# Expert gathers of a decoder layer in chunks of 8 slots: another distance between the two streams, twelve diagonals, other work moved between the first slots

## The reference

```
q = h @ w_q                                  # 8 heads, 2 parts of 128
s = q . sub_keys                             # 128 keys per head and part
s1, i1 = top_k(s[part 0], 16); s2, i2 = top_k(s[part 1], 16)
top_s, e = top_k of the 256 sums s1 + s2     # 16 experts per head, e = i1 * 128 + i2
g = softmax(top_s)
act = gelu(u_tab[e] . h)
y = sum over 8 x 16 experts of (g * act) * v_tab[e]
out = x1 + gate2 * y
```

## Time and profile before

| | |
|---|---|
| median of 3 runs | 1356.63 us |
| the profiled execution | 1362.06 us |
| its span | 1360.4 us |
| busy: PE / DVE / ACT / POOL | 1060.8 / 705.3 / 244.3 / 655.7 us |
| mean granted clock of PE | 0.884 of full |
| read from HBM | 377.55 MB, of them 302 MB for the 576 gathers |
| first gather / last gather asked | 486.75 / 1335.20 us |

### The profile page before, as it was taken

One profiled execution on the slowest core, in us unless ns is written; L12 is line 12 of the kernel. 1 busy time (PEld: TensorE's weight loads), 2 busy tenths in 40 slices (PEclk: granted clock), 3 DMA queues, 4 the chain that ended last, 5 costly groups with the idle time before them and its releaser, 6 DMA issues.

```text
span 1360.4 us, 12692 instructions
## 1 busy us (share of the span) xinstructions
PE 1060.8 (78%) x3429; PEld 568.0 (42%) x3429; DVE 705.3 (52%) x1695; ACT 244.3 (18%) x552; POOL 655.7 (48%) x787
## 2 busy tenths in 40 slices
PE   6898888996899979657776768776857777777797
PEld 3346666664676766323322323232322333233243
DVE  3157453886142366768467466473772774334421
ACT  1011121123201103111121211211202112112021
POOL 3333334331000043667666667566666666666651
PEclk9798898998999999879878988788889888987799
DMA  7653241885043474899999999999999999999993
GB/s 237 203 191 113 73 134 46 285 289 146 1 153 133 179 305 141 330 370 369 366 370 368 367 365 367 355 368 374 365 376 379 353 368 370 364 382 352 373 372 118
DMA packets 126411, 379.87 MB, mean 279 GB/s; under 512 B 14284, under 2 KB 23624, under 8 KB 126356
## 3 DMA queue, kind: packets, MB, share of 16 engines
q0 software_dynamic: 89408, 312.89, 61.3%
q1 hardware_dynamic: 36948, 66.29, 14.6%
HBM read 377.55 MB, written 1.59 MB: 279 GB/s over the span
## 4 chain that ended last, share of the span: by engine, by line
PE 65%; issue 15%; DVE 8%; another core or an unknown queue 5%; ACT 4%; DMA 2%; POOL 1%; SPq 0%; DVEq 0%; ACTq 0%
PE twoD L825 19%; PE twoD L827 17%; PE twoA L513 6%; PE twoA L779 4%; PE twoD L730 2%; PE twoA L490 2%; PE twoA L653 1%; PE twoD L608 1%; PE twoA L450 1%; PE twoD L720 1%; PE twoD L696 1%; PE twoD L466 1%; DMA big<-w_ada 1%; DVE big L1593 1%
## 5 line engine op out<-in xcount | busy, mean ns | idle before, releaser
L825 PE MATMUL twoD<-big 128*128 128x512 f32 x576 | 344.7, 684 | 204.6 <-issue 184.5
L951 POOL DMA_INDIRECT big<-peer_v,oT x288 | 273.0, 948 | 179.4 <-issue 79.9
L827 PE MATMUL twoD<-big 128*128 128x512 f32 x576 | 327.5, 653 | 0.0
L938 POOL DMA_INDIRECT big<-peer_u,oT x210 | 199.6, 950 | 247.9 <-DVEq L1551 163.9
L825 PEld LDWEIGHTS twoD<-big 128*128 128x128 f32 x576 | 114.7, 213 | 391.3 <-issue 387.7
L1182 ACT ACTIVATE big<-ctab,oT 128x128 f32<-128x128 f32 x288 | 110.1, 399 | 640.0 <-remote 257.9
L827 PEld LDWEIGHTS twoD<-big 128*128 128x128 f32 x576 | 122.4, 213 | 163.7 <-issue 163.7
L1593 DVE CUSTOM_DVE_ANT_0 big<-big,twoA 128x1024 f32<-128x1024 f32 x115 | 137.3, 1217 | 69.9 <-DMA big<-peer_u,oT 56.0
L1593 DVE CUSTOM_DVE_ANT_0 big<-big,twoD 128x1024 f32<-128x1024 f32 x95 | 114.6, 1215 | 40.4 <-DMA big<-peer_u,oT 23.7
L513 PE MATMUL twoA<-hT,big 128*128 128x288 f32 x448 | 114.3, 415 | 0.0
L513 PEld LDWEIGHTS twoA<-hT,big 128*128 128x128 f32 x448 | 86.0, 194 | 24.2 <-issue 0.8
(11 more groups left out here) (285 smaller groups left out, 1004.3 us busy)
## 6 DMA issues: line engine op xcount, KB each, us to landing
big<-w_ada SPq DMA_DIRECT2D x12, 2048.0 KB, 9.2
big<-w_in SPq DMA_DIRECT2D x5, 2048.0 KB, 8.1
big<-w_in SPq DMA_DIRECT2D x9, 1024.0 KB, 11.3
big<-peer_w_q SPq DMA_DIRECT2D x4, 2048.0 KB, 8.0
big<-peer_v,oT POOLq DMA_INDIRECT x288
big<-cache_v POOLq DMA_DIRECT2D x64, 64.0 KB, 2.1
big<-w_out SPq DMA_DIRECT2D x2, 2048.0 KB, 7.8
big<-cache_k POOLq DMA_DIRECT2D x56, 64.0 KB, 3.6
```

Source lines behind the costliest of these rows:

```text
L825: pe.matmul(acc[0][:, :], diag[:, j % NDG, :], row[:, 0:512], start=(s == 0), stop=(s == SLOTS[t] - 1), skip_group_check=True)
L827: mm = pe.matmul(acc[1][:, :], diag[:, j % NDG, :], row[:, 512:D], start=(s == 0), stop=(s == SLOTS[t] - 1), skip_group_check=True)
L938: pool.indirect_dma_start(urows[i % NU], None, peer_u, bass.IndirectOffsetOnAxis(ap=eidx[:, t, s:s + 1], axis=0)).then_inc(u_in[i % NU], 16)
L951: pool.indirect_dma_start(vrows[j % NV], None, peer_v, bass.IndirectOffsetOnAxis(ap=eidx[:, t, s:s + 1], axis=0)).then_inc(v_in[j % NV], 16)
```

## The change

Sizes: chunks of 8 slots (`CHUNK`) in place of 16 for gelu, weighting and `w_ready`; NU 11 to 10, NV 10 to 11, NDG 4 to 12 (the further diagonals lie in tensors that are no longer in use). The v stream runs behind the u stream by `min(18, 10 + i // 8, 8 + (287 - i) // 3)` slots: 10 at first, 18 from slot 64, and down to 8 at the last slot.

Order: the gate2 rows, the later scores and the token rows become 15 pieces `late(k)` that PE makes before v slots 6, 8, ..., 34, in the order g2, scores, token rows, and ACT copies after the diagonal six slots later. h of tiles 1 and 2 is turned before slot 64. `gelus(c + 1)` stands behind diagonal 8c + 7, `exps` behind the gelu of every fourth chunk, and `normalise` inside `weigh`, which DVE comes to at i = 11, 19, ...

Storage: the last group of q weights has a place of its own, so its load no longer waits for the second group's use; the stores of the convolution state and the load of the bias stand earlier in SP's order.

```
-        NU, NV = 11, 10
+        NU, NV = 10, 11
-        LAG = 24
-        HEAD = PTOP
+        LAG, NEAR = 18, 8
+        HEAD, CHUNK = PTOP, 8
+        NDG = 12
...
+        slot_of[-1] = 4
+        shares = {0: (0, 2, 3), 1: (1,), 2: (0, 2), 3: (0, 3), 4: (4,)}
...
+        LATE = list(range(6, 6 + 2 * 15, 2))
+        H2_REST = 64
...
             for j, (t, s) in enumerate(slots):
+                if j in LATE:
+                    late(LATE.index(j))
+                if j == H2_REST:
+                    pe.wait_ge(a_free, A.n)
+                    turn_h2(1)
+                    turn_h2(2)
...
-            for i in range(ROUNDS + LAG):
-                if i < ROUNDS:
-                    ask_u(i)
-                if i >= LAG:
-                    ask_v(i - LAG)
+            asked = 0
+            for i in range(ROUNDS):
+                ask_u(i)
+                lag = min(LAG, NEAR + 2 + i // 8, NEAR + (ROUNDS - 1 - i) // 3)
+                while asked <= i - lag:
+                    ask_v(asked)
+                    asked += 1
+            for j in range(asked, ROUNDS):
+                ask_v(j)
...
             for j, (t, s) in enumerate(slots):
-                c = j // HEAD
-                if j % HEAD == HEAD - NDG and (c + 1) * HEAD < ROUNDS:
-                    if c % 2 == 0 and c // 2 + 1 < len(pairs):
-                        exps(c // 2 + 1)
-                    gelus(c + 1)
-                if j % HEAD == 0:
+                c = j // CHUNK
+                if j % CHUNK == 0:
                     act.wait_ge(w_ready, c + 1)
                 if j >= NDG:
                     act.wait_ge(v_used, j - NDG + 1)
-                act.activation(diag[:, j % NDG, :], ident, ACT.Copy, scale=dots[:, t, s:s + 1]).then_inc(diag_ready, 1)
+                act.activation(diag[j % NDG], ident, ACT.Copy, scale=dots[:, t, s:s + 1]).then_inc(diag_ready, 1)
+                if j - 6 in LATE:
+                    late(LATE.index(j - 6))
+                if j % CHUNK == CHUNK - 1 and j + 1 < ROUNDS:
+                    gelus(c + 1)
+                    if c % 4 == 1 and (c + 3) // 4 < len(pairs):
+                        exps((c + 3) // 4)
...
             def weigh(c):
+                if c % 4 == 0:
+                    normalise(c // 4)
...
                 dot(i)
-                if i % (2 * HEAD) == HEAD // 2:
-                    normalise(i // (2 * HEAD))
-                if i % HEAD == 1 and i >= HEAD:
-                    weigh(i // HEAD - 1)
+                if i % CHUNK == 3 and i >= CHUNK:
+                    weigh(i // CHUNK - 1)
```

More of the change, by code:

```diff
@@ L785, in _, with late @@
             score_bank(0, 3)
[L787 to L791, removed]
+            def late(k):
+                if k < 4:
+                    if k == 0:
+                        pe.wait_ge(bias_landed, 16)
+                        pe.wait_ge(g2sel_ready, 1)
+                    half, s = k // 2, k % 2
+                    pe.wait_ge(adaG_ready, half + 1)
                     b = A.open(pe)
                     pe.matmul(b[:, :], g2sel[:, s * P:(s + 1) * P], adaG[:, half, :], start=True, stop=False)
-                    mm = pe.matmul(b[:, :], ones[0:1, :], biasG[:, half * 512:(half + 1) * 512], start=False, stop=True)
+                    A.close(pe.matmul(b[:, :], ones[0:1, :], biasG[:, half * 512:(half + 1) * 512], start=False, stop=True))
+                elif k < 8:
+                    score_bank(1, k - 4)
+                elif k == 8:
+                    b = A.open(pe)
+                    for r in range(4):
+                        for i in range(4):
+                            hp = 4 * r + i
+                            mm = pe.matmul(b[32 * r:32 * r + 32, i * P:(i + 1) * P], qpT[:, hp, SEQ:TOK],
+                                           subT[:, (hp % 2) * PH + hp // 2, :], start=True, stop=True)
                     A.close(mm)
-            for t in range(3):
-                for half in range(2):
+                else:
+                    t, half = (k - 9) // 2, (k - 9) % 2
                     b = A.open(pe)
@@ L824, in _ @@
                 row = vrows[j % NV]
-                pe.matmul(acc[0][:, :], diag[:, j % NDG, :], row[:, 0:512], start=(s == 0), stop=(s == SLOTS[t] - 1),
+                pe.matmul(acc[0][:, :], diag[j % NDG], row[:, 0:512], start=(s == 0), stop=(s == SLOTS[t] - 1),
                           skip_group_check=True)
-                mm = pe.matmul(acc[1][:, :], diag[:, j % NDG, :], row[:, 512:D], start=(s == 0), stop=(s == SLOTS[t] - 1),
+                mm = pe.matmul(acc[1][:, :], diag[j % NDG], row[:, 512:D], start=(s == 0), stop=(s == SLOTS[t] - 1),
                                skip_group_check=True)
@@ L1563, in weigh @@
             def weigh(c):
-                t, first = slots[c * HEAD]
+                if c % 4 == 0:
+                    normalise(c // 4)
+                t, first = slots[c * CHUNK]
                 dve.wait_ge(gelu_done, c + 1)
-                chunk = dots[:, t, first:first + HEAD]
-                L.tell(tt(chunk, chunk, gate[:, t, first:first + HEAD], ALU.mult), w_ready, wait=False)
+                chunk = dots[:, t, first:first + CHUNK]
+                L.tell(tt(chunk, chunk, gate[:, t, first:first + CHUNK], ALU.mult), w_ready, wait=False)
             def output(t):
```

85 lines of the change are left out of this document (40 added, 45 removed).

## The result

The changed kernel takes 1336.7 us (median of 4 runs, 1334.6 to 1340.3), the kernel before beside it 1357.7 us: 0.985 of it, interval 0.982 to 0.988. The forecast was 1302 us. A gain of 21 us came where 55 were forecast. The profiled execution took 1336.01 us.

A forecast was written before the change was run, and what follows sets the result against it. The kernel was taken as bound by a gather stream stopped now and then by late news of used slots. Span 1360.4 - 20 (start) - 31 (middle) - 4 (end) = 1305.4 us, so a median of 1302 us; range 1240 to 1338.

The forecast's parts named there:

- The start: First 34 asks: moving DVE's two waits to dot 11 brings the 35th ask to about 539 us; 20 us gained.
- The middle: From 559 to 1297 us: more spare slots make POOL's stops rarer, 1.427 to 1.367 us an ask; 31 us gained.
- Rival (b): Middle: late news lasts until any ring is full, pace stays 1.427 us, only start and end gain; 1333 us, chance 0.20.
- a price of the full stream: Middle: the assumed reason why news of finished slots reaches POOL and ACT late, some 17 us.
- Rival (a): Middle: diagonals and eleventh v row swallow every late time, asks run at 1.27 us; 1252 us, chance 0.25.
- DVE's visits: Middle: DVE's waits for a gelu double from 18 to 36, but most should find it ready; costed at nothing.
- Rival (c): Middle: DVE's handshake with ACT makes the kernel slower, past 9.1 us a visit; 1410 us at 10.7, chance 0.08.
- The forecast's count of spare slots: DVE's visits for a gelu: the slot needed lies 24 back instead of 26, leaving 6 to spare instead of 2.
- Rival (d): Middle: the fewer u rows stop POOL as often as v did, so no change; 1357 us, chance 0.05.
- The end: From 1297 us: last 24 asks go at the middle's pace, 24 to 25 us still follow the last; 4 us gained.
- The last step of the sum: From the profiled execution, 1307 us, to the median of the runs, 5.4 us lower: 1302 us.
- PE's clock: PE slots: idle gaps could leave PE cold, 3.5 us a slot; put in the range, not made a case.

The follow-up runs named there:

- e2: Changed kernel with the 15 late pieces and the second and third part of h2 back in front of the first v slot and first gelu; 1357.6 us, 1.001.
- e8: Changed kernel with PE raising the count of used v slots only behind every second slot, on the chip without late news; 1258.7 us, 0.989 of the kernel before.
- e16: Changed kernel with a ring of 8 v rows instead of 11, u keeping 10, on a chip with late news; 1334.4 us, 0.982 of the kernel before.
- e7: Changed kernel with asks of 128 rows of 2 KB instead of 4 KB, half of each dot left out; 1338.4 us, 0.981 of the kernel before.
- e18: Changed kernel with asks of 64 rows instead of 128, other partitions' work left out, on a chip with late news; 1335.1 us, 0.985 of the kernel before.
- e11: Changed kernel with asks of 64 rows instead of 128, other partitions' work left out, on the chip without late news; 1242.9 us, 0.977 of the kernel before.
- e5: Changed kernel with a short pause on POOL after each ask (a memset of one element per partition and a wait); 1356.2 us, 0.993 of the kernel before.
- e6: Changed kernel with a longer pause on POOL after each ask (a memset of 64 elements per partition); 1350.9 us, 0.991 of the kernel before.
- e1: Changed kernel with 4 diagonal buffers instead of 12, all else as changed; 1367.6 us, 1.009 of the kernel before.
- e3: Changed kernel with v asked 24 behind u from first ask to last, without the nearer distance at both ends; 1358.1 us, 1.001 of the kernel before.
- e10: Changed kernel with DVE raising the count of used u rows only behind every second dot, on the chip without late news; 1258.1 us, 0.988.
- e4: Changed kernel with chunks of 16 slots and v at most 24 and at nearest 14 behind u, 12 diagonals kept; 1330.3 us, 0.981 of the kernel before.

## Why the prediction was right or wrong

**The start, 20 us forecast, 14.3 measured: the place right, the size off.** The waits did move to i = 11, the 35th ask came before 545 us (at 544.97, just), no gap reached 15 us, and e2 shows that the pieces' place carries the gain: back in front they cost 22.6 us. The term was too large because I let the late news out of it. I had ACT's exponentials end at 529.65 as before and DVE go on at 534; they ended at 538.7, and DVE's `weigh(0)` stood at 540.32. The last pair of q copies had waited 14.99 us and came at 533.36, though PE had finished them by 525.7. Before the change the same copies came on time:

```profile
525.77 0.41 ACT L1139 ACTIVATE r<-twoA 128x288 f32<-128x288 f32 x1 [3.47 <-PE twoA L779]
```

Before, POOL stood still from 517.6 to 532.61 us; in the changed kernel it asked without a break until 530.4. So filling POOL's time there seems to have made the news late on which the exponentials wait; e8, where the same asks run without late news, agrees. Without late news (e8) the 35th ask is 43.2 us behind the first, better than my forecast of 52. The first v slot was at 541.06, where I had said before 540.

**The middle, 31 us forecast, 7.8 measured: this step failed.** "so four spare slots last some 15 us and eight some 29. A cycle of 15 + 15 us of asking and 4 us of stop becomes 15 + 29 and 4." The kernel did get its spare slots and PE did follow the landings, but the stops kept their sum: 85 us against 90. Counting pauses up to five asks apart as one, there were 20 of over 1.5 us instead of 25, and each was longer, 4.2 against 3.4 us on average; 22 of 3.7 us with eight rows. Eight v rows (e16) gave 82 us, thirteen 92, four diagonals 112 in all. In no version on the chips with late news did the sum fall under 82 us, unless POOL paused by itself. The time from one stop to the next rose from some 30 to 37 us, where the forecast had it rise from 34 to 48, but the stops grew with it; and with eight rows it was 34 us, so three rows fewer hardly shortened it. Rival (b) had this in so many words, "the late time grows until any ring is full, and the pace stays": 1333 us forecast for it, 1336.7 measured, chance given 0.20. I took one place at 853 us for a rate of news (one slot in 7 to 10 us) and multiplied it, though the rows of 22 slices, all alike, stood against it.

**Its reason was wrong too.** I named the late news "a price of the full stream". e7 and e18 move half of the bytes and have all of it; e8 runs at 409 GB/s for 600 us and has none. What the runs show is this: in five of six sets of runs, on at least four chips, and not on the chip of e8 to e11, PE's news comes late while POOL asks without a pause, and comes some 4 us after POOL stops. Since a pause by choice replaces most of a stop (e5, e6) and stops of u replace stops of v (e1, e3), what seems to change little is how much POOL stands still per ask, pauses counted in: 0.16 to 0.19 us in most versions, 0.20 in e5 and e6, 0.22 in e1. That is argued from the sums, not shown.

**Rival (b)'s page.** By the Trainium skill, DMA: Bandwidth & Descriptors, section "Where 436 GB/s comes from", the HBM side binds at about 358 GB/s, and the middle's 370 would be its limit. The runs disagree twice: 184 GB/s gave the same pace (e7), and 409 GB/s was held for 600 us (e8). Rival (b) came true without its page's reason.

**Rival (a)**, the full stream at 1.27 us an ask, is what a chip without late news gives, 1258 us against my 1252; but the kernel before also gets most of it there (1273.8 us). The change seems worth some 15 us there instead of 21, by e8 to e10, which differ from it in messages alone; the changed kernel itself did not run on that chip, and the kernel before has no trace from it.

**DVE's visits, costed at nothing: right, 40.8 us in 36, 1.1 us each**, by the reason given, the spare slots, and e1 and e3 show that this was worth saying: with either part taken back it is 7.9 and 7.0 us a visit, and e1 is slower than before. Rival (c) was a real mechanism that two parts of the change hold down, though its price of 9.1 us a visit was not reached. The forecast's count of spare slots parts the runs: six to spare in the changed kernel and eight in e4 (1.1 us a visit each); two before (8.6), none in e3 (7.0), two too few in e1 (7.9). Rival (d) fell.

**The end, 4 us forecast, 4.3 measured: the number came true by luck.** Nine v asks do follow the last u. But the forecast had the last 24 asks speed up from 1.56 us each to the middle's pace and the time from the last ask to the end stay at 24 to 25 us. The 24 asks took 1.53 us each, 0.8 us gained, and the time behind the last ask fell from 25.2 to 20.9.

**The last step of the sum**, 5.4 us off because the traced execution before lay so far above its median, was no property of the kernel: the changed one lay 0.7 us below its own.

**PE's clock** was no trouble: 0.94 granted in the middle instead of 0.84, and 1.00 without late news.

Open: what holds the news back, why only on some chips, and whether it is held back when nothing is recorded. Longer pauses at fewer places were not tried, nor an ask whose landing raises its count fewer times.

## What to carry to other kernels

Where two engines wait for a third one's count and are let go in the same instant, don't size rings by the rate of news seen there: first take rows away, then bytes, and see whether the sum of the stops moves. Edits to one handshake are bound together: here diagonals and distance each undid the whole when taken back alone (e1, e3), while chunks and distance taken back together cost nothing (e4), so price them as one wait (which slot must be used when this visit comes) and not as a list. And run the kernel before beside every version: between chips it differed by up to 92 us, four times the gain. Look, too, whether a trace holds all records of the counts on which a reading of "remote" rests.

## What was unexpected of the hardware

- The kernel before took 1356 to 1365 us on several chips and 1273.8 us on one. By the traces of the changed kernel's versions the difference is in the time in which POOL gathers: the first ask comes at 484 to 491 us on all, a middle ask takes some 1.42 or 1.27 us.
- On the chips with late news PE's semaphore updates reached ACT and POOL up to 23 us late while POOL asked back to back, and DVE's own reached DVE up to 8.7 us late (e7). In the same traces two thirds or more of the records of landings are missing from the time of the gathers. Twice or half as many updates of PE made no difference (0.984, 0.985), nor did half of the bytes or half of the rows per ask.
- One core held 409 GB/s of gathered 4 KB rows for 600 us.
- An indirect ask of 64 rows costs POOL 0.91 us of work, one of 128 rows 0.94, and one of 128 rows of 2 KB 0.95 to 0.96.
